# Hybrid Fourier and dilated-attention encoder block on 8 cores: norm scaling handed out in steps between matmul tiles, first loads in another order with sums on two engines, rotary rows gathered in two parts

## The reference

```python
h = rms_norm(x, norm_mix)
x = x + hybrid_mixer(h, ...)      # 2-D DFT branch + dilated attention branch, gated, one projection
x = x + memory_cross_attention(rms_norm(x, norm_cross), rms_norm(mem, norm_mem), ...)
a = relu(rms_norm(x, norm_mlp) @ w_up);  x = x + (a * a) @ w_down
return rms_norm(x, norm_final)
# in the mixer: u, q, k, v and two gates = h @ w_in;  q and k of 12 heads get a rotary turn of their
# first 16 of 64 dims; three head groups attend with (window, dilation) = (128,1), (512,4), (2048,16)
```

## Time and profile before

| | us |
|---|---|
| median of 3 runs (2214.08 to 2215.31) | 2214.44 |
| the profiled execution | 2214.59 |
| its span on the slowest core, core 0 | 2213.4 |
| spans of the 8 cores | 2197.1 to 2213.4 |
| TensorE busy in it | 1993.7 (90%) |
| DVE, ACT, POOL busy | 1007.8, 759.9, 420.3 |

### The profile page before, as it was taken

How to read it: one execution, slowest core, us unless ns; L and a number is a source line. 1 busy time by engine, 2 the same in 40 slices (tenths; PEclk the granted TensorE clock), 3 DMA queues, 4 the chain that set the end, 5 groups by cost and what they waited for, 6 DMA issues and landing times.

```text
span 2213.4 us, 30436 instructions; the slowest of 8 cores (2197.1 to 2213.4 us)
## 1 busy us (share of the span) xinstructions
PE 1993.7 (90%) x10053; PEld 974.7 (44%) x10232; DVE 1007.8 (46%) x1581; ACT 759.9 (34%) x1259; POOL 420.3 (19%) x380
## 2 busy tenths in 40 slices
PE   2579968999999999999988896899999999999996
PEld 1245533455444444444334454344544444444443
DVE  3654554345454333333667355633555533333346
ACT  3334434234543111113533443523455311111143
POOL 2500002344131000002542000234412300000031
PEclk9789989999999999999999998999999999999998
DMA  7431224245402222222244322232550004040203
GB/s 189 122 77 30 58 48 152 39 77 92 80 1 77 38 39 39 39 39 39 96 141 136 78 66 58 96 95 56 98 95 1 1 1 77 3 75 3 56 39 115
DMA packets 30474, 147.02 MB, mean 66 GB/s; under 512 B 4465, under 2 KB 8690, under 8 KB 20082
## 3 DMA queue, kind: packets, MB, share of 16 engines
q0 software_dynamic: 11808, 75.50, 19.2%
q1 hardware_dynamic: 18514, 69.57, 9.6%
HBM read 197.48 MB, written 16.78 MB: 97 GB/s over the span
## 4 chain that ended last, share of the span: by engine, by line
PE 76%; DVE 8%; issue 4%; ACT 4%; DMA 3%; POOL 2%; SPq 2%; DVEq 0%; ACTq 0%; POOLq 0%
PE ps L149 76%; DVE arena L149 8%; ACT arena L149 4%; POOL arena L149 2%; DMA arena<-arena 2%; SPq L147 2%; DMA arena<-x 1%; DVEq L143 0%; ACT L149 0%; ACTq L143 0%; SPq L149 0%; POOLq L143 0%; SPq L143 0%
## 5 line engine op out<-in xcount | busy, mean ns | idle before, releaser
L149 PE MATMUL ps<-arena 128*128 128x512 bf16 (+3 forms) x10053 | 1993.7, 359 | 212.9 <-ACT arena L149 90.5
L149 PEld LDWEIGHTS ps<-arena 128*128 128x128 bf16 (+2 forms) x10232 | 974.7, 101 | 1231.6 <-issue 314.5
L149 ACT ACTIVATE arena<-ps 128x512 bf16<-128x512 f32 (+4 forms) x774 | 475.4, 631 | 1042.7 <-PE ps L149 902.5
L149 DVE TENSOR_TENSOR arena<-arena 128x512 bf16<-128x512 bf16 (+7 forms) x610 | 306.3, 523 | 648.2 <-ACT arena L149 628.7
L149 POOL TENSOR_TENSOR arena<-arena 128x512 f32<-128x512 f32 (+2 forms) x288 | 366.0, 1272 | 754.8 <-ACT arena L149 461.6
L149 DVE TENSOR_TENSOR arena<-ps,arena 128x512 f32<-128x512 f32 (+3 forms) x376 | 294.2, 790 | 270.4 <-PE ps L149 268.9
L149 ACT ACTIVATE arena<-arena 128x512 f32<-128x512 f32 (+3 forms) x440 | 260.7, 599 | 355.3 <-DVE arena L149 224.1
L149 DVE SCALAR_TENSOR_TENSOR arena<-arena 128x512 bf16<-128x512 f32 (+3 forms) x288 | 219.0, 831 | 72.8 <-ACT arena L149 72.8
L149 POOL DMA_DIRECT2D arena<-wb x62 | 33.7, 545 | 785.8 <-PE ps L149 721.1
L149 DVE SCALAR_TENSOR_TENSOR arena<-arena,ps 128x512 f32<-128x512 f32 x128 | 82.1, 683 | 152.0 <-PE ps L149 151.8
L149 DVE SCALAR_TENSOR_TENSOR arena<-ps,arena 128x512 f32<-128x512 f32 x64 | 42.6, 685 | 26.9 <-PE ps L149 26.9
(11 more groups left out here) (3 smaller groups left out, 0.3 us busy)
## 6 DMA issues: line engine op xcount, KB each, us to landing
arena<-wb POOLq DMA_DIRECT2D x62, 1024.0 KB, 9.3
arena<-x SPq DMA_DIRECT2D x8, 2048.0 KB, 13.3
arena<-x SPq DMA_DIRECT2D x28, 512.0 KB, 8.0
out<-arena SPq DMA_DIRECT2D x28, 512.0 KB, 2.8
arena<-wa POOLq DMA_DIRECT2D x20, 512.0 KB, 9.1
arena<-rope SPq DMA_DIRECT2D x6, 1024.0 KB, 9.5
arena<-arena SPq DMA_DIRECT2D x96, 64.0 KB, 2.6
arena<-dft SPq DMA_DIRECT2D x2, 2048.0 KB, 12.8
```

What stands on the lines that cost most here:

```text
L149: ins = getattr(eo, o['name'])(*o['args'], **o['kw'])
```

## The change

Four things. (1) The norms in `pend` become generators: one step is the statistics (`norm_rstd`), and each of 8 further steps one STT; `popp` takes 2 steps at each of the units fc 3 to 7 (4 steps in the last MLP pass of the first sequence). The denominators of cross-attention (`den`) come one unit later, and half of the copies of `kp_gen` go from DVE to ACT. (2) The first sequence starts with x on SP, the constants on ACT's queue, weight loads one by one on POOL's; x has four buffers; the squares of the first four tiles are summed by DVE (even chunks) and POOL (odd chunks) into two sums; the read-out of q and k in this stage is all ACT's; where each norm stands among the 6 units of a tile is written out in a table of hooks. (3) The second sequence takes all 6 units of a tile together, its last input tile uses the other set of sums. (4) `gather` is called for q and for k apart, q's during the k projections, and the rows come back in two groups of 4 DMAs with a semaphore each, c = 0 first.

The lines of the start of `norm_sq` (`isinstance(eng, int)`), of the first sequence's start, of its table of hooks and of the rotary, among others; `load_consts` squares one number on ACT, issues cb, gains, fmix and altrow from there, and casts fmix:

```diff
-        def popp(fc):
-            if fc in (3, 6) and pend:
-                pend.pop(0)()
+        def popp(fc, first=3, steps=2):
+            n = steps if fc >= first else 0
+            while n and pend:
+                if next(pend[0], 0) is None:
+                    n -= 1
+                else:
+                    pend.pop(0)
...
             def fin_norm(gi, tg):
-                def f():
-                    norm_rstd()
-                    norm_apply(gi, [xT[:, tg, c, :] for c in range(8)],
-                               [hT[:, c, tg * 512:(tg + 1) * 512] for c in range(8)])
-                return f
+                norm_rstd()
+                yield
+                for c in range(8):
+                    stt(hT[:, c, tg * 512:(tg + 1) * 512], xT[:, tg, c, :], gains[:, gi, c:c + 1], rstd, ALU.mult, ALU.mult)
+                    yield
...
+            if isinstance(eng, int):
+                sq4 = sq + wide[eng][2:]
+                odd = wide[eng][ns][:, 0:n]
+                part = (acc_, odd)[k % 2]
+                b = sq4[k % 4][:, 0:n]
+                act(part if k < 2 else b, src, AF.Square)
+                if k > 1:
+                    tt(('dve', 'pool')[k % 2], part, part, b, ALU.add)
+                if k == 7:
+                    tt('dve', acc_, acc_, odd, ALU.add)
+                    act(hi, acc_, AF.Copy)
+                    tt('dve', lo, acc_, hi, ALU.subtract)
+                return
...
             if b_ == 0:
                 load_xin(0, 0, 0, 256)
                 aload(0)
+                load_consts()      
                 load_xin(0, 0, 256, 256)
+                load_xin(0, 1, 0, 256)
+                load_xin(0, 1, 256, 256)
+                for h in range(2):
+                    norm1_sq(0, 0, ns=h, t0=h * 256, n=256, eng=0)
+                    norm1_fin(0, 0, h, h * 256, 256)
+                    wk = aload(1 + h)
+                load_xin(0, 2, after=[wk])
+                load_xin(0, 3)
                 load_rope(0)
...
+                for tg, t0, n, hooks in (
+                        (0, 0, 256, {3: [lambda: sq1(0)]}),
+                        (0, 256, 256, {1: [lambda: sq1(1)], 2: [lambda: fin1(0)], 5: [lambda: fin1(1)]}),
+                        (1, 0, 256, {0: [lambda: norm1_sq(0, 2, eng=0)]}),
+                        (1, 256, 256, {3: [lambda: norm1_fin(0, 2)]}),
+                        (2, 0, 512, {0: [lambda: norm1_sq(0, 3, eng=0)], 3: [lambda: norm1_fin(0, 3)], 5: [make_wz]}),
+                        (3, 0, 512, {0: [lambda: v_ones(0), load_dft, mem_sq]})):
...
+            def gather(g, which):
+                rows = rot_rows(g, which, 0) + rot_rows(g, which, 1)
+                OP('sp', 'dma_group', rows, reads=[qkv_views(g)[which]], writes=[rot], dma_key='rg%d' % which)
...
-                OP('sp', 'dma_group', list(zip(rows, tmp)), reads=[rot], writes=rows, dma_key='rb')
+                for c in range(2):
+                    pairs = [(r, t) for which in range(2) for t, r in rot_rows(g, which, c)]
+                    q_, k_, _ = qkv_views(g)
+                    OP('sp', 'dma_group', pairs, reads=[rot], writes=[q_[:, c, :], k_[:, c, :]], dma_key='rb%d' % c)
```

More of the change, by code:

```diff
@@ L62, in res, with op @@
         return out
-    def op(self, eng, name, *args, reads=(), writes=(), dma_key=None, **kw):
+    def op(self, eng, name, *args, reads=(), writes=(), dma_key=None, after=(), **kw):
         i = len(self.ops)
@@ L71, in op @@
             wset |= set(self.res(a))
-        deps = set()
+        deps = set(after)
         for k in rset:
@@ L258, in mm, with dma @@
             OP('pe', 'matmul', out, lhsT, rhs, start=start, stop=stop, reads=[lhsT, rhs], writes=[out], **kw)
-        def dma(q, out, in_, key):
-            OP(q, 'dma_start', out=out, in_=in_, reads=[in_], writes=[out], dma_key=key)
+        def dma(q, out, in_, key, after=()):
+            return OP(q, 'dma_start', out=out, in_=in_, reads=[in_], writes=[out], dma_key=key, after=after)
         def act(out, in_, func, scale=1.0, bias=None):
@@ L265, in act @@
             reads = [in_]
+            if not isinstance(scale, float):
+                reads.append(scale)
             if bias is not None:
@@ L303, in build_program @@
         rstd = view(T0 + 8192, 512, F32)
+        wide = [[view(o + i * 2048, 512, F32) for i in range(4)] for o in (OFF['X'] + 52 * 1024, OFF['Y'])]
         hT = view(OFF['hT'], 8 * 2048, pat="p (c t) -> p c t", c=8)
@@ L485, in qk_unit, with rot_rows @@
                 cp(eng, o_, o.rearrange("p (j r) -> p r j", r=dil))
[L489 to L496, removed]
+            def rot_rows(g, which, c):
+                t = qkv_views(g)[which]
+                return [(rot[i * 16:(i + 1) * 16, :], t[p0:p0 + 16, c, :])
+                        for i, p0 in ((4 * which + 2 * c, 0), (4 * which + 2 * c + 1, 64))]
+            def gather(g, which):
+                rows = rot_rows(g, which, 0) + rot_rows(g, which, 1)
+                OP('sp', 'dma_group', rows, reads=[qkv_views(g)[which]], writes=[rot], dma_key='rg%d' % which)
             def rotate(g):
-                rows, tmp = rot_rows(g)
                 OP('dve', 'stream_shuffle', rsw, rot, SHUF, reads=[rot], writes=[rsw])
@@ L782, in proj_gen @@
                     if n == 7:
+                        gather(g, 0)
                         if g == 1:
@@ L985, in out_gen @@
                     norm_sq(fc, x_)
+                    while dens:
+                        dens.pop(0)()
                     popp(fc)
@@ L1015, in up @@
                     if nxt is not None:
-                        norm1_sq(nxt, [fc], ns=1)
-                    popp(fc)
+                        norm1_sq(b_ + 1, nxt, [fc], ns=1)
+                    popp(fc, 3, 4 if p_ == 3 and not last_seq else 2)
             def down(p_, tg, t0=0, n=512):
@@ L1061, in fin_next @@
             def fin_next(tg, b_=b_):
-                def f():
-                    norm1_fin(tg, 1)
-                    if tg < 2:
-                        load_xin(b_ + 1, tg + 2)
-                return f
+                norm_rstd(ns=1)
+                yield
+                for c in range(8):
+                    stt(hT[:, c, tg * 512:(tg + 1) * 512], xin[tg % 2][:, c, :], gains[:, 0, c:c + 1], rstd, ALU.mult, ALU.mult)
+                    yield
+                if tg < 2:
+                    load_xin(b_ + 1, tg + 2)
             def nxt(tg):
```

177 lines of the change are left out of this document (84 added, 93 removed).

## The result

The changed kernel takes 2147.48 us (median of 4 runs, 2145.21 to 2147.99), the kernel before, run beside it, 2214.49 (2214.08 to 2215.31). The ratio is 0.9695 [0.9678, 0.9712], 67 us less; forecast were 2142 us and 2112 to 2180.

What follows compares the result with a forecast made beforehand. TensorE was taken as the bound, busy 90% of the span, so at most 220 us could come from closing its pauses. Terms 25 + 23 + 19 + 4 + 1.5 = 72.5 off 2214.6 gave 2142 us, range 2112 to 2180.

Steps and rivals of the forecast that it cites:

- The start: First sequence's opening norms: the memory's scaling block at 101.5 instead of 126.0 us, 25 us less (8 to 45).
- the two rounds: Start, tiles 2 and 3: each a loop from a tile's first unit to the next tile's, 18.6 us, twice 37.
- the memory: Last link of the start: the memory's load, squares, read-outs, Ln and Exp take 15 us.
- arrival of x: Start: three weight loads fewer beside x, 3 x 3.3 = 10 us less; first square taken at 10.5 us.
- The bound of 15 us: Start: first square at 15 us at worst, if fmix lands 9.9 us after a table load.
- That each link of the loop needs the one before it: Start's rounds: argument against the rival that they shrink by 10 us each (2122 us, chance 0.12).
- The two sides of the SBUF: Start: by the skill's exclusion rule split sums partly queue, about 1 us more per norm, gain 21 instead of 25.
- The rotaries: Row copies before attention: half of 43.0 us of waits goes (21), plus 2 from the gather; 23 us less (8 to 30).
- The norms in the middle: Cross-attention of both sequences: stepped scalings remove 90% of 10.4 + 10.9 us idle, 19 us less (5 to 24).
- the slower rival: Stepped norms: scalings among POOL's additions take 1386 ns everywhere, 90 us lost, 2251 us in all; chance 0.05.
- Between the sequences: Passage from first to second sequence: 4.65 us pauses stay, half of 9.42 goes, new waits come; 4 less.
- The end: Kernel's tail: POOL sums again, 14 additions leave DVE, scalings come singly; 1.5 us less (3 more to 4 less).

Runs made afterwards that it cites:

- e_fmix: ACT's cast of fmix moved from ahead of the first square to make_wz, against the changed kernel: ratio 0.9674 to before, die span 2136.9 us.
- e_sq3: Tile 3's squares issued right after tile 2's statistics instead of behind tile 2's first unit, against the changed kernel: ratio 0.9655 to before, die span 2137.4 us.
- e_quiet2: Loads wb 0, wb 1, wb 4 and next rotary tables wait for the second group of rows back, against the changed kernel: ratio 0.9611 to before, die span 2119.3 us.
- p_rot: Kernel before with the rotary part alone (gather in two calls, rows back in two groups of four copies): ratio 0.9858 to before, die span 2179.2 us.

## Why the prediction was right, point by point

*The start* (forecast 25): 21.4 to the memory's block, 23 as a part by itself. Link by link: first block at 21.6 for 18; to the end of tile 1's first unit (47.95 + 3.25 + 0.3) 29.9 for 31.5; the two rounds, each to a unit's end in the same way, 20.7 and 18.3 for 18.6, the first longer since the block of tile 1's second half (5.29 us at 52.45) stands on DVE ahead of tile 2's sums; the memory 14.0 for 15. From the first block to the memory's the chain took 82.9 us where 83.5 were forecast. The mis-sized term is *arrival of x*: squares near 10.5 were forecast, 14.2 measured. I had taken 3 x 3.3 us off one arrival, but the block needs the last of four pieces, which lands at 14.6 (e_fmix) even where fmix holds nobody. The bound of 15 us was nearer.

*That each link of the loop needs the one before it*: by the queues' order, yes. e_sq3 shows how little is gained by moving one link.

*The two sides of the SBUF.* The scalings of 512 columns at the start take 746 ns on average (1386 in the earlier trace rows), where POOL's sums no longer run beside them; DVE's additions, which belong to the same sums as POOL's, 885:

```profile
L149 DVE SCALAR_TENSOR_TENSOR arena<-arena 128x512 bf16<-128x512 f32 x16 | 10.8, 746 | 5.5 <-ACT arena L149 5.5
...
L149 DVE TENSOR_TENSOR arena<-arena 128x512 f32<-128x512 f32 x8 | 7.1, 885 | 6.1 <-ACT arena L149 3.3 <-POOL arena L149 2.4 <-DVE arena L149 0.2
```

This mean hides two kinds. Six of the eight additions start while POOL isn't adding and take 0.69 us each; two start while it adds and take 1.28 and 1.66. The first of these beside POOL's addition, and one of the eight scalings at 1117.72 beside another:

```profile
75.38 1.28 POOL L149 TENSOR_TENSOR arena<-arena 128x512 f32<-128x512 f32 x1 [14.28 <-ACT arena L149]
75.93 1.28 DVE L149 TENSOR_TENSOR arena<-arena 128x512 f32<-128x512 f32 x1 [0.41 <-ACT arena L149]
...
1118.11 1.49 POOL L149 TENSOR_TENSOR arena<-arena 128x512 f32<-128x512 f32 x1 [1.75 <-ACT arena L149]
1118.38 1.75 DVE L149 SCALAR_TENSOR_TENSOR arena<-arena 128x512 f32<-128x512 f32 x1
```

DVE's instruction ends about 0.55 us after POOL's (77.21 and 76.66; 1120.13 and 1119.60), as if it had done most of its work only then. The same holds for 18 of the 24 scalings behind the 1386 ns of the earlier trace rows, which is such a mixed mean too. The rule of the Trainium skill ("SBUF — State Buffer", section "SBUF: two separate sides"), that a DVE instruction with two SBUF inputs and a POOL instruction that reads SBUF exclude each other for their whole duration, fits these rows: the trace agrees with it wherever two of them meet. What decides is how often they meet.

By the rule the prediction put the gain of the start at 21 instead of 25, and 21.4 came; that this is near is luck in part. The meetings cost 0.9 us in tile 0's first block (4.19 instead of 3.25), 2.0 in the second block of tile 1 (5.29), 1.6 in tile 3's additions and 0.3 in each of six additions of half tiles, some 6 together where about 4 were counted. But the chain behind the first block was 0.6 us shorter than a forecast that left them out, so other links were sized too long or lay off the chain; what is missing from the 25 lies at x.

*The rotaries* (forecast 23, 21 of it by the two groups): the waits fell by 19.4, and putting the single semaphore back costs 20.8. The cause that I gave, copies that land late behind weight loads, is shown by e_quiet2. What the forecast left out is that the remaining half goes too once the loads wait. The term was too small: p_rot alone gives 27, and in the ledger below these stretches give 29.

*The norms in the middle* (19): idle time fell by 15.5 us in the two stretches, from 10.4 and 10.9 to 2.9 each; on core 1 by 13.8, of which the steps carry 9.8. "90%" was too much; one pause of 2.7 us is left in each sequence, ended by ACT; its cause was not looked into. The mean of the scalings is within the 0.7 to 0.9 us that decided against the slower rival, because only five of these 48 start while POOL adds (1.20 us on average), the others taking 0.75:

```profile
L149 DVE SCALAR_TENSOR_TENSOR arena<-arena 128x512 bf16<-128x512 f32 x48 | 36.2, 792 | 6.1 <-ACT arena L149 5.9
```

*Between the sequences* (4): next to nothing was gained. The pauses that were to stay stayed (4.65 to 4.95), of 9.42 there are 3.31 left, and the new ones of "some 5" and 3 came as 5.13 and 3.87. Counted between the same weight loads on core 1, from the last pass of the MLP to just before the end of the next sequence's u, q and k units, the passage takes 119.59 us before and 120.50 after:

```profile
1072.47:1192.06 119.59, 97.01 (x402) 40.58 (x401) 78.53 (x109) 48.02 (x86) 57.21 (x49) 0.89 0.50 145
...
1028.15:1148.65 120.50, 95.04 (x402) 40.26 (x401) 86.38 (x119) 48.13 (x86) 57.09 (x49) 0.93 0.49 144
```

TensorE's idle time grew from 22.6 to 25.5 us; the busy time of the same 402 matmuls fell by 2.0, at a granted clock of 0.93 instead of 0.89. On the eight cores the passage comes out between 1.3 us longer and 1.7 shorter. So the pauses were foreseen one by one, but their sum is not a gain of 4.

*The end* (1.5): nothing. 6.30 became 5.10, but the wait of the last statistics grew from 5.21 to 6.17; from the same weight load (before 2154.42, now 2087.21) the program takes 59.0 us to its end in both.

*The ledger.* On the slowest core, the same places in both traces: the memory's block comes 21.44 us earlier; the first matmul behind TensorE's pause ahead of the gates 34.67 (347.75, now 313.08); a weight load at the start of the passage 44.04 (1078.87, now 1034.83); the first v unit of the second sequence 42.83 (1201.15, now 1158.32); the first matmul behind the pause ahead of its gates 58.76 (1413.39, now 1354.63); and the program's end 67.2 (2213.4, now 2146.2). The differences from place to place, by term:

| term | forecast | measured |
|---|---|---|
| start | 25 | 21.4 |
| rotaries, with the attention around them | 23 | 13.2 + 15.9, in sum 29.2 |
| norms in the middle | 19 | 9.4 + 8.4, in sum 17.8 |
| between the sequences | 4 | -1.2 |
| end | 1.5 | 0 |

The sum of 72.5 came out as 67 since these misses partly cancel: the rotaries gave 6 us more than forecast, the start 4 and the passage 5 less. The three large terms had their mechanisms right; that the total is this near is in part luck.

## What to carry to other kernels

Before moving a small, late-needed copy, look at what else is on the DMA engines when it is issued: here loads of which the weights weren't due for 100 us and more cost 19 us. A load is held back by a wait on the copy, not by a later place in the program, when its queue is empty. Steps between tiles paid in the cross-attention; in the passage, where DVE has more to do, they moved the pauses and gained nothing. Before taking a mean duration as the price of two engines working side by side, look at single instructions: there were two kinds, those that met and those that didn't.

## What was not expected of the hardware

A 64 KB copy of rows landed a median of 2.3 us after its issue with the engines quiet, and 10.2 beside two 1 MB weight loads. Eight scalings beside seven additions of POOL took 12.45 us, 5.39 by themselves: a DVE instruction that starts while POOL adds ends 0.55 us after POOL's addition. A granted clock of 0.977 instead of 0.964 made 13.7 of the 69.5 us on core 1, with 50 matmuls more.
